# Making one weight sum of each gate/up pair with an adding DMA, and alternating four plain halves instead of three with the products

## What is computed

```python
D_MODEL = 2048
SEQ = 256
FFN_HIDDEN = -(-8 * D_MODEL // (3 * 256)) * 256
...
def _swiglu(x, w_gate, w_up, w_down):
    return (jax.nn.silu(x @ w_gate) * (x @ w_up)) @ w_down
...
        x = _layer_norm(DEEPNORM_ALPHA * x + m, ln1_g, ln1_b)
        x = _layer_norm(DEEPNORM_ALPHA * x + _swiglu(x, w_gate, w_up, w_down), ln2_g, ln2_b)
```

## Time and profile before

| | us |
|---|---|
| median of 3 runs | 934.3 (933.99 to 934.36) |
| the profiled execution: its own time | 934.59 |
| the profiled execution: its span | 932.8 |
| PE busy | 924.1 |
| DVE busy | 775.2 |
| ACT busy | 514.1 |
| POOL busy | 95.8 |

### The profile page before, as it was taken

How to read it: one execution, slowest core, us unless ns; L and a number is a source line. 1 busy time by engine, 2 the same in 40 slices (tenths; PEclk the granted TensorE clock), 3 DMA queues, 4 the chain that set the end, 5 groups by cost and what they waited for, 6 DMA issues and landing times.

```text
span 932.8 us, 11643 instructions
## 1 busy us (share of the span) xinstructions
PE 924.1 (99%) x4406; PEld 774.2 (83%) x4406; DVE 775.2 (83%) x1049; ACT 514.1 (55%) x704; POOL 95.8 (10%) x84
## 2 busy tenths in 40 slices
PE   9999999999999999999999999999999999999997
PEld 8999988888878888888888888888887788888885
DVE  6778566578779898989999898988969997799777
ACT  5686765353464646555564646555545564456550
POOL 0205530000311020202111030000000000000000
PEclk9999999999999999999999999999999999999999
DMA  9844324584707475665748375665666656355532
GB/s 362 318 160 151 121 91 178 183 342 167 302 20 274 129 255 174 212 217 166 246 120 288 115 254 165 234 203 180 230 235 257 227 223 237 124 217 234 229 132 91
DMA packets 36759, 188.06 MB, mean 202 GB/s; under 512 B 4064, under 2 KB 4576, under 8 KB 22880
## 3 DMA queue, kind: packets, MB, share of 16 engines
q1 hardware_dynamic: 36672, 187.32, 56.2%
q0 software_dynamic: 32, 0.00, 0.0%
HBM read 183.11 MB, written 4.19 MB: 201 GB/s over the span
## 4 chain that ended last, share of the span: by engine, by line
PE 96%; DVE 3%; ACT 0%; issue 0%; DVEq 0%; ACTq 0%
PE acc L1982 26%; PE acc L2004 19%; PE acc L1757 9%; PE tp L1982 9%; PE acc L1965 6%; PE acc L1695 5%; PE tp L1965 4%; PE acc L1616 4%; PE tp L2004 3%; PE acc L1894 2%; PE tp L1934 2%; DVE w_lo L1423 2%; PE acc L1729 1%; PE tp L1808 1%; PE tp L1743 1%; DVE turned L1352 1%
## 5 line engine op out<-in xcount | busy, mean ns | idle before, releaser
L1982 PE MATMUL acc<-w_hi,act_t 128*128 128x512 f32 x720 | 227.4, 389 | 0.0
L971 ACT ACTIVATE w_hi<-raw 128x1024 fp32r<-128x1024 f32 x120 | 125.9, 1058 | 111.0 <-PE acc L1982 53.2
L1020 ACT ACTIVATE w_hi<-raw 128x512 fp32r<-128x512 f32 (+1 forms) x154 | 115.2, 782 | 100.8 <-PE acc L2004 82.7
L2004 PE MATMUL acc<-w_hi,hid_t 128*128 128x512 f32 x504 | 161.5, 390 | 1.5 <-DVE w_lo L1423 1.5
L1423 DVE TENSOR_TENSOR w_lo<-raw,w_hi 128x512 fp32r<-128x512 f32 (+1 forms) x154 | 132.1, 881 | 35.3 <-ACT w_hi L1020 34.8
L1982 PEld LDWEIGHTS acc<-w_hi,act_t 128*128 128x128 f32 x720 | 135.1, 188 | 28.1
L1376 DVE TENSOR_TENSOR w_lo<-raw,w_hi 128x1024 fp32r<-128x1024 f32 x120 | 147.9, 1249 | 7.7 <-ACT w_hi L971 6.8
L1982 PE MATMUL acc<-w_lo,act_t 128*128 128x512 f32 x360 | 140.0, 389 | 0.0
L2004 PEld LDWEIGHTS acc<-w_hi,hid_t 128*128 128x128 f32 x504 | 94.6, 188 | 22.1 <-DVE w_lo L1423 2.3
L2004 PE MATMUL acc<-w_lo,hid_t 128*128 128x512 f32 x252 | 98.0, 389 | 0.0
L1373 DVE TENSOR_TENSOR w_lo<-raw,w_hi 128x1024 fp32r<-128x1024 f32 x63 | 82.7, 1313 | 17.7 <-ACT w_hi L966 17.5
(11 more groups left out here) (262 smaller groups left out, 1581.9 us busy)
## 6 DMA issues: line engine op xcount, KB each, us to landing
raw<-in_w_pairs SPq DMA_DIRECT2D x120, 512.0 KB, 4.6
raw<-in_w_down SPq DMA_DIRECT2D x44, 1024.0 KB, 5.3
raw<-in_w_pairs SPq DMA_DIRECT2D x18, 1024.0 KB, 7.8
raw<-in_w_out SPq DMA_DIRECT2D x16, 1024.0 KB, 4.9
raw<-in_w_gu SPq DMA_DIRECT2D x8, 1024.0 KB, 10.5
raw<-in_x_w SPq DMA_DIRECT2D x14, 552.0 KB, 7.1
raw<-in_w_uq SPq DMA_DIRECT2D x4, 1024.0 KB, 7.5
raw<-in_w_ukv SPq DMA_DIRECT2D x4, 1024.0 KB, 6.0
```

The lines of the kernel that those rows point to most:

```text
L971: act.activation(w_hi[:, v % RING, :], plain_raw(m), ACT.Copy).then_inc(hi_done, 1)
L1020: act.activation(unit_parts(u)[0], block_of(b, block, width), ACT.Copy).then_inc(down_hi_done, 1)
L1982: last = pe.matmul(out[:, t, :], act_t[:, k0 + m, x, t * P:(t + 1) * P], part[:, v % RING, m * GC:(m + 1) * GC], start=False, stop=(end an ...
L2004: last = pe.matmul(bank, lhs(x), part[:, cols * GC:(cols + 1) * GC], start=(first == u and (cols, x) == (0, 0) and part is hi_), stop=(end ...
```

## The change

The DVE instruction that makes T1 is gone. In its place GpSimd issues one DMA for each pair (`load_t1`): it reads b12 again from the weights in device memory, 128x2x512 float32 or 512 KB, and adds it to `B11` in SBUF. It waits until DVE has made the low part of P1, and it raises a new semaphore, `t1_full`, on which ACT waits before it splits T1 for P5. GpSimd's loop over the hidden sums is cut into two functions, and the DMA of pair p stands ahead of the low part of p-2 and the sums of p-1.

The order of the steps is changed too: P2 moves from behind P7 to the place behind P1, and four plain halves of the preceding pair alternate with P1, P2, P5 and P6, where three alternated with P1, P5 and P6. The seed from P1 is now awaited by P2. T4 is now made after P6's low part, since P2 stands ahead of P5.

```diff
-        ends = [(p - 1, "second", n) for n in range(PLAIN - 3, PLAIN)] if p > 1 else [None] * 3
-        for product, end in zip((P1, P5, P6), ends):
+        ends = [(p - 1, "second", n) for n in range(PLAIN - 4, PLAIN)] if p > 1 else [None] * 4
+        for product, end in zip((P1, P2, P5, P6), ends):
             steps += [(p, "product", product), end]
-        steps += [(p, "product", n) for n in (P7, P2, P3)] + [(p, "first", 0), (p, "product", P4)]
-        steps += [(p, "first", n) for n in range(1, PLAIN)] + [(p, "second", n) for n in range(PLAIN - 3)]
+        steps += [(p, "product", n) for n in (P7, P3)] + [(p, "first", 0), (p, "product", P4)]
+        steps += [(p, "first", n) for n in range(1, PLAIN)] + [(p, "second", n) for n in range(PLAIN - 4)]
...
+                    elif n == P5:
+                        act.wait_ge(t1_full, 16 * p)
                     elif n in SUM_OF:
-                        act.wait_ge(pair_t_done, 4 * (p - 1) + SUM_OF[n] + 1)
+                        act.wait_ge(pair_t_done, 3 * (p - 1) + SUM_OF[n])
...
                 if (kind, n) == ("product", P1):
-                    pair_sum(p, B11, B11, B12)
                     pair_sum(p, B12, B12, B22)
                 if (kind, n) == ("product", P5):
                     pair_sum(p, B11, B11, B22)
-                if (kind, n) == ("product", P2):
+                if (kind, n) == ("product", P6):
                     pair_sum(p, B21, B11, B21)
...
+            def load_t1(p):
+
+                pool.wait_ge(lo_done, V_OF[p, "product", P1] + 1)
+                b12 = by_quad(w_pairs[p - 1][:, 0:2 * RAW_ELEMS])[:, :, B12 * GC:(B12 + 1) * GC]
+                pool.dma_start(quad(p, B11), b12, accum_op=ALU.add).then_inc(t1_full, 16)
+
+            def factor_sums(q):
+
...
+            def factor_low(q):
+
                 pool.wait_ge(s_hi, q + 1)
                 pool.tensor_tensor(s_t[:, q, 1, :, :], s_sum[:], s_t[:, q, 0, :, :], ALU.subtract).then_inc(s_lo, 1)
+
+            for p in range(1, PAIRS):
+                load_t1(p)
+                if 0 <= p - 2 < len(DOWN_QUADS):
+                    factor_low(p - 2)
+                if p - 1 < len(DOWN_QUADS):
+                    factor_sums(p - 1)
...
-                if n in (P6, P7, P4):
-                    pe.wait_ge(seeded, 3 * p - 2 + (P6, P7, P4).index(n))
+                if n in (P2, P7, P4):
+                    pe.wait_ge(seeded, 3 * p - 2 + (P2, P7, P4).index(n))
```

More of the change, by code:

```diff
@@ L155, in ffn_sequence @@
     for p in range(1, PAIRS):
-        ends = [(p - 1, "second", n) for n in range(PLAIN - 3, PLAIN)] if p > 1 else [None] * 3
-        for product, end in zip((P1, P5, P6), ends):
+        ends = [(p - 1, "second", n) for n in range(PLAIN - 4, PLAIN)] if p > 1 else [None] * 4
+        for product, end in zip((P1, P2, P5, P6), ends):
             steps += [(p, "product", product), end]
-        steps += [(p, "product", n) for n in (P7, P2, P3)] + [(p, "first", 0), (p, "product", P4)]
-        steps += [(p, "first", n) for n in range(1, PLAIN)] + [(p, "second", n) for n in range(PLAIN - 3)]
-    steps += [(PAIRS - 1, "second", n) for n in range(PLAIN - 3, PLAIN)]
+        steps += [(p, "product", n) for n in (P7, P3)] + [(p, "first", 0), (p, "product", P4)]
+        steps += [(p, "first", n) for n in range(1, PLAIN)] + [(p, "second", n) for n in range(PLAIN - 4)]
+    steps += [(PAIRS - 1, "second", n) for n in range(PLAIN - 4, PLAIN)]
     return tuple(step for step in steps if step)
@@ L472, in layer_kernel @@
         pair_t_done = sem("pair_t_done")
+        t1_full = sem("t1_full")
         seeded = sem("seeded")
@@ L1581, in _ @@
             a11, a12, a21, a22 = (turned[:, 0, c, t * P:(t + 1) * P] for t in range(TOK) for c in range(2))
-            for q in range(len(DOWN_QUADS)):
+            def load_t1(p):
[3 more added lines that the diff above has]
+            def factor_sums(q):
                 if q > 0:
```

## The result

The changed kernel takes 941.53 us in the median of 4 runs (941.15 to 941.82) against 934.33 us (933.99 to 934.76) of the kernel before: 7.2 us slower, a ratio of 1.0075 with a 95% interval of 1.0063 to 1.0087. The forecast was 938.1 us, with a range of 935.8 to 946.0.

What follows compares the result with a forecast made beforehand. PE was taken as the bound, busy 422.33 of the stage's 423.00 us. 0 (DVE) + 3.8 (pair 1) + 0 (pairs 2 to 10) on the 934.3 median gave 938.1 us, range some 935.8 to 946.

Steps and rivals of the forecast that it cites:

- PE is the bound and DVE's time is free: Ten-pair stage: no matmul waits for DVE, so removing ten DVE sums, 12.2 us, is worth nothing on the path.
- Pair 1 pays X - 1.8 us: Pair 1: P2 waits for a seed queued behind the splits of P5 and P6; 3.7 us at X = 5.5.
- X: Time from DVE having made P1's low part to T1 lying in SBUF; taken as 5.5 us in pair 1.
- floor of 1.3 us: Pair 1: the least P2 waits however fast the DMA, since P5's ring place opens only at 266.8.
- The sum as a whole: Whole kernel: 0 for DVE, +3.8 us for pair 1, 0 for pairs 2 to 10, making 938.1 us.
- 0.1 for a slow first matmul behind a wait: Pair 1, behind P2's wait: 0.1 us added, as P7's first matmul took 0.50 instead of 0.39.
- Pairs 2 to 10 hide the DMA: Pairs 2 to 10: plain halves and early issue cover the DMA, so it costs 0 at X = 5.5 or 6.5.
- the limit at X = 7.0 to 7.8: Pairs 2 to 8: the largest X that costs nothing, 4.1 plus 2.9 us or 7.8; taken as 7.4.
- the seed from P7: Pairs 2 to 10, ahead of (first, 0): ACT's seed done at 18.6 against 19.1, the smallest margin found, 0.5 us.
- the rival of a late T1: Every pair: from X = 7.4 each microsecond costs one in about seven pairs; X = 8 gives +10.5 us; chance 0.25.
- The relative of that rival: Pair 1: GpSimd cannot issue while DVE runs, making the sum 5.0 to 6.2 us instead of 3.8; no separate chance.
- The rival of a DMA as quick as a plain load: Pair 1: adding is free, X is 3.3 or less, P2 waits 1.3 to 1.5 us, total within 0.2%; chance 0.12.

Runs made afterwards that it cites:

- order-only run: Changed kernel's new step order with no adding DMA, DVE making T1 in every pair, against the kernel before: 935.68 us, ratio 1.0012.
- run with DMAs in pairs 2 to 10: Changed kernel, but DVE makes T1 in pair 1 and the adding DMA stays in the other pairs: 936.09 us, ratio 1.0015.
- Half the bytes: Changed kernel with the adding DMA covering only the first of two depth quads, 256 KB instead of 512: 937.41 us in one run.
- filler run: Changed kernel with 17 unused matmuls added on PE between P1 and P2 of pair 1: 939.41 us, ratio 1.0050.
- late-issue run: Kernel with the adding DMA only in pairs 2 to 10, its DMA issued one low part later: 958.0 us against 936.09 without the delay.
- old order: Adding DMA in every pair, but with the step order of the kernel before: 976.51 us, ratio 1.0450.
- plain copy: Changed kernel with GpSimd's DMA only copying b12 over B11, adding nothing: 938.72 us, ratio 1.0041.

## Why the prediction was right or wrong

**PE is the bound and DVE's time is free: right.** The order-only run and the run with DMAs in pairs 2 to 10 differ by 12 us of DVE work and by 0.4 us of time.

**Pair 1 pays X - 1.8 us: right to a tenth.** In the kernel after X was 269.75 - 263.40 = 6.35, which gives some 4.5; P2 was 4.52 late. Half the bytes gave 4.54 and 2.71. The floor of 1.3 us was measured as 1.3 as well.

**X = 5.5: too low.** Landing took 6.0 to 6.3 us, and 0.3 lie between the low part and the issue. I had taken the low end of SP's 1 MB loads plus GpSimd's 0.4, which is 5.2, and put it at 5.5, because pair 1's queues are empty. The empty queues made no difference: 6.03 in pair 1, 6.1 in the median. What I lacked is that adding makes GpSimd itself slower (1.2 us against the 0.73 of the earlier trace rows), and the 0.3 us up to the issue. This term was short by 0.8 us.

**The sum as a whole: half of what was measured, by a term that was missing.** It had P2's wait and 0.1 us for a slow first matmul. The 2.8 us behind it were not in it: the granted clock at 0.50 for some 6 us of matmuls. The step that fell short is "0.1 for a slow first matmul behind a wait", which was read off a wait of 0.67 us and laid on one of 3.7; slow matmuls behind the wait cost 2.9. No wait of this stage of the kernel before brought the clock down, so no row there could show that this would happen. The slow pitch itself does stand in that trace, among PE's first matmuls:

```profile
4.29 1.19 PE L1616 MATMUL acc<-in_hi 128*128 128x512 f32 x2
5.28 0.92 PE L1616 MATMUL acc<-in_hi,in_lo 128*128 128x512 f32 x2
6.04 0.63 PE L1616 MATMUL acc<-in_lo,in_hi 128*128 128x512 f32 x2
```

Two matmuls take 0.99 and 0.76 us there from start to start, and two take 0.47 right behind them (6.04 to 6.51). I took the pitch of 0.227 us as given. The filler run shows the term by taking it away.

**Pairs 2 to 10 hide the DMA: right, with less room than I said.** I put the issue 2.9 us ahead of P1 on PE and the limit at X = 7.0 to 7.8. The issue came 2.3 us ahead (306.28 against 308.62), behind GpSimd's hidden sums as forecast, and the limit on P5's split is the lower of my two values, 4.1 us behind P1. So from issue to landing there were 6.4 us and not 7.4, and 6.0 to 6.3 were used. The lower value holds since in pairs with GpSimd's low part T2 takes 2.04 us instead of 1.22. DVE in the kernel after (start, length, instruction):

```profile
313.70 1.23 DVE L1376 TENSOR_TENSOR w_lo<-raw,w_hi 128x1024 fp32r<-128x1024 f32 x1 [2.49 <-ACT w_hi L969]
314.84 2.04 DVE L1383 TENSOR_TENSOR raw<-raw 128x1024 f32<-128x1024 f32 x1
316.80 1.22 DVE L1379 TENSOR_TENSOR w_lo<-raw,w_hi 128x1024 fp32r<-128x1024 f32 x1
```

and on PE:

```profile
318.14 0.43 PE L2002 MATMUL acc<-w_hi,act_t 128*128 128x512 f32 x1
```

The last low part ends at 318.02 and PE takes it at 318.14, so 0.1 us were left. I had called the seed from P7, with 0.5 us, the tightest spot; that seed cost nothing, and the tight spot was this one. It was luck, by some tenth of a microsecond, that the rival of a late T1, worth 22 us in the late-issue run and 42 in the old order, did not come true. Its price was too low: it began at 7.4, and in the late-issue run the DMA that was issued later also landed later after its issue.

**The relative of that rival, GpSimd held up by DVE: wrong here.** The DMA was issued 0.3 us behind P1's low part while DVE went on with T3 (263.32 to 264.54) and landed after 6.03 us, no later than elsewhere. DVE was at work beside the other DMAs too, so a small cost is not ruled out. The Trainium skill, page "SBUF — State Buffer", section "SBUF: two separate sides", says that a DVE operation on two SBUF inputs blocks only a GpSimd operation that reads SBUF. The trace agrees on both sides: the DMA was issued and landed in 6.03 us beside T3, and T2 took 2.04 us instead of 1.22 beside GpSimd's subtraction (314.17 to 315.80).

**The rival of a DMA as quick as a plain load: wrong.** It decided at X = 3.6, and X was 6.35; even the plain copy from GpSimd took 4.3 us. The Trainium skill, page "DMA: Bandwidth & Descriptors", section "Anatomy of one DMA — SWDGE (gpsimd) path", gives 2.0 us plus bytes by 436 GB/s, an estimate of 3.2 us for 512 KB. That is too low for both: the measured times are 4.3 us for the copying DMA and 6.1 for the adding one.

## What to carry to other kernels

Where one engine is busy for 422 of 423 us, time taken off another is worth nothing, and what replaces it must be priced by its latency at the place with the least cover, here the first pair, where no work of a preceding pair stands between the products. A new wait of the matrix engine can have a second price behind it, the time at half clock (2.9 us behind 4.4 here, none behind 2.55); where the trace has no idle time of that length, it belongs in the range as a term of its own. An operation that is hidden "with room" should be checked against the spot next to it too: the first matmul that needs it had 1.9 us, the one behind it 0.1.

## What the runs showed of the hardware

- An adding DMA of 512 KB issued by GpSimd takes 6.1 us to land, a copying one 4.3, an adding one of 256 KB 4.3; GpSimd is busy with it for 1.20, 0.72 and 0.86 us. With empty queues the adding one took 6.03 us, beside SP's loads 6.0 to 6.3 in the changed kernel; issued 1.7 us later, 0.3 to 0.5 us behind a load of SP, it took 7.2.
- The granted clock of the matrix engine fell to 0.50 in an idle time of 4.4 us and came back after some 6 us of matmuls, most of them 0.43 us apart, a price of 2.9 us. Seventeen matmuls that serve nothing, put into the idle time, kept it at 1.00.
- Behind an idle time of 2.61 us it fell in the profiled run of the plain copy, and in another run of that kernel, with a mean clock of 1.00, it did not; it did not in that of the half-size DMA (2.55 us). With the DMA in the old order it fell at idle times of 1.96 and 1.29 us close together in pair 4 and not at 1.89 and 1.36 in pair 3. So the length of the idle time alone does not tell. Why, these runs leave open.
- A DVE sum of 128x1024 on two SBUF inputs took 2.04 us instead of 1.22 beside a subtraction of GpSimd; GpSimd's DMA was issued 0.3 us after the low part that it waited for, though DVE was at work.
